# Two diffusion-backbone layers on one core: the experts as one run of slices, the pair gather inside the pair ahead, and identity products in PE's waits

## The reference

```
def _moe(h, router, wg, wu, wd):
    logits = (h @ router).astype(jnp.float32)
    top_v, top_i = lax.top_k(logits, TOP_K)
    w = jax.nn.softmax(top_v, axis=-1)
    combine = jnp.sum(jax.nn.one_hot(top_i, N_EXPERTS) * w[..., None], axis=-2)
    for e in range(N_EXPERTS):
        out = out + combine[..., e:e + 1] * _swiglu(h, wg[e], wu[e], wd[e])
```

## Time and profile before

| | us |
|---|---|
| median of 3 runs | 1887.31 |
| lowest, highest | 1887.2, 1889.62 |
| the profiled execution, its own time | 1881.97 |
| its span on the core | 1880.1 |
| PE busy | 1794.9 (95%) |
| PE weight loads | 1463.5 (78%) |
| DVE busy | 1333.4 (71%) |
| ACT busy | 1049.5 (56%) |
| POOL busy | 121.3 (6%) |

### The profile page before, as it was taken

One profiled execution on the slowest core, in us unless ns is written; L12 is line 12 of the kernel. 1 busy time (PEld: TensorE's weight loads), 2 busy tenths in 40 slices (PEclk: granted clock), 3 DMA queues, 4 the chain that ended last, 5 costly groups with the idle time before them and its releaser, 6 DMA issues.

```text
span 1880.1 us, 21725 instructions
## 1 busy us (share of the span) xinstructions
PE 1794.9 (95%) x8804; PEld 1463.5 (78%) x8804; DVE 1333.4 (71%) x1245; ACT 1049.5 (56%) x989; POOL 121.3 (6%) x128
## 2 busy tenths in 40 slices
PE   4999989999999999887999999999999999999998
PEld 2986578888888878666888888888888888888886
DVE  2478656332333457745989988999888998898988
ACT  3333744222222244454777777777777777777774
POOL 1020900000000012321000000000000000000000
PEclk8999989999999999997999999999999999999999
DMA  8325913522433133654899998999999999999994
GB/s 296 129 90 188 350 63 77 141 90 82 109 95 101 40 118 129 217 210 179 301 374 378 360 375 324 367 375 362 375 328 361 376 360 375 332 360 374 369 368 165
DMA packets 246198, 472.80 MB, mean 251 GB/s; under 512 B 10578, under 2 KB 60596, under 8 KB 246092
## 3 DMA queue, kind: packets, MB, share of 16 engines
q1 hardware_dynamic: 242000, 468.14, 69.9%
q10 hardware_dynamic: 4092, 3.20, 0.6%
HBM read 470.26 MB, written 1.05 MB: 251 GB/s over the span
## 4 chain that ended last, share of the span: by engine, by line
PE 89%; DVE 5%; ACT 2%; DMA 2%; issue 1%; POOL 1%; SPq 0%; ACTq 0%; POOLq 0%; DVEq 0%
PE bank L554 26%; PE bank L556 26%; PE bank L555 26%; DMA raw<-in_ada_w_dram 2%; PE bank L572 2%; DVE parts L1749 1%; PE bank L1116 1%; PE bank L801 1%; PE bank L1063 1%; PE bank L790 1%; PE bank L782 1%; PE bank L1076 1%; ACT parts L1310 1%; PE bank L851 1%; PE bank L733 1%
## 5 line engine op out<-in xcount | busy, mean ns | idle before, releaser
L1764 DVE TENSOR_TENSOR expert_low<-expert_loaded,expert_high 128x2048 fp32r<-128x2048 f32 x336 | 765.5, 2289 | 84.8 <-ACT expert_high L1451 84.5
L1451 ACT ACTIVATE expert_high<-expert_loaded 128x2048 fp32r<-128x2048 f32 x336 | 642.8, 1919 | 194.5 <-PE bank L556 194.5
L554 PE MATMUL bank<-expert_high,XEr 128*128 128x512 f32 x896 | 354.7, 396 | 6.8 <-issue 4.1
L556 PE MATMUL bank<-expert_high,XEr 128*128 128x512 f32 x896 | 349.9, 390 | 0.0
L555 PE MATMUL bank<-expert_low,XEr 128*128 128x512 f32 x896 | 349.6, 390 | 0.0
L1310 ACT ACTIVATE parts<-raw 128x2048 fp32r<-128x2048 f32 (+1 forms) x62 | 113.2, 1831 | 269.8 <-PE bank L556 249.7
L1749 DVE TENSOR_TENSOR parts<-raw,parts 128x2048 fp32r<-128x2048 f32 (+1 forms) x62 | 135.7, 2193 | 136.3 <-ACT parts L1310 136.0
L554 PEld LDWEIGHTS bank<-expert_high,XEr 128*128 128x128 f32 x896 | 168.7, 188 | 42.3 <-issue 9.1
L556 PEld LDWEIGHTS bank<-expert_high,XEr 128*128 128x128 f32 x896 | 168.5, 188 | 35.6
L555 PEld LDWEIGHTS bank<-expert_low,XEr 128*128 128x128 f32 x896 | 168.8, 188 | 33.5
L554 PE MATMUL bank<-expert_high,HTr 128*128 128x512 f32 x448 | 174.5, 390 | 0.0
(11 more groups left out here) (246 smaller groups left out, 2236.6 us busy)
## 6 DMA issues: line engine op xcount, KB each, us to landing
expert_loaded<-in_moe_w_gate_dram SPq DMA_DIRECT2D x112, 1024.0 KB, 5.5
expert_loaded<-in_moe_w_up_dram SPq DMA_DIRECT2D x112, 1024.0 KB, 5.5
expert_loaded<-in_moe_w_down_dram SPq DMA_DIRECT2D x112, 1024.0 KB, 5.2
raw<-in_ada_w_dram SPq DMA_DIRECT2D x28, 1024.0 KB, 7.8
more<-in_ada_w_dram SPq DMA_DIRECT2D x20, 1024.0 KB, 7.8
raw<-in_w_in_dram SPq DMA_DIRECT2D x12, 1024.0 KB, 5.1
raw<-in_ffn_w_gate_dram SPq DMA_DIRECT2D x22, 512.0 KB, 3.9
raw<-in_ffn_w_up_dram SPq DMA_DIRECT2D x22, 512.0 KB, 5.2
```

Of the source, the lines that this page charges most:

```text
L554: nc.tensor.matmul(out, st[0], mv[0], start=start, stop=False)
L556: return nc.tensor.matmul(out, st[1], mv[0], start=False, stop=stop)
L1451: nc.scalar.activation(high[:, m % PARTS, :], loaded[:, at, :], ACT.Copy).then_inc(hi_ready, 1)
L1764: return nc.vector.tensor_tensor(out, a, b, op)
```

## The change

- **One run of experts.** The four pairs of 14 slices become one run of 56 (`slices`), with items and semaphore counts numbered through. The order within a slice is kept. The end of a pair is gone as a place of its own.
- **The gather inside the pair ahead.** `gathers_in` puts the gather of pair p in slices 10 and 11 of pair p-1: in slice 10 its left half (16 products) between the turn and up, in slice 11 its right half, both into banks M. ACT brings the left half out in slice 10, DVE the right half in slice 11, and the second half of the high and low parts is made in slice 12. The first pair's gather stays ahead of the experts.
- **Identity products.** `keep_busy` issues n plain products of the identity by itself (128x128, float32) into a bank that nobody reads: 9 ahead of the last values of each attention, then 8 (layer 0) or 11 (layer 1); in the routing chain 8 ahead of the second tile's turn, 6 behind it, 11 ahead of the ranks, 5 ahead of the first gather, 9 behind it.
- **POOL** waits ahead of its first `xnr` until DVE has emptied the bank of the second tile's turn.

```diff
+            def keep_busy(out, n):
+
+                for _ in range(n):
+                    nc.tensor.matmul(out, ident, ident, start=True, stop=True)
...
+                    if m == last + 1:
+                        spare = (turn_v[0] + 1) % ring_v[0]
+                        pe.wait_ge(v_done, user_v[spare] + 1)
+                        keep_busy(VB[spare][:, 0:P], 9)
                     if m >= 2:
                         values(2 * m - 4)
                         values(2 * m - 3)
+                    if m == last + 1:
+                        keep_busy(VB[spare][:, 0:P], 8 if layer == 0 else 11)
...
                     if t:
+                        keep_busy(b[:, P:2 * P], 8)
                         turn_routed(1, banks)
+                        keep_busy(b[:, P:2 * P], 6)
...
                 b = open_v()
+                keep_busy(b[:, P:2 * P], 11)
                 after(mask_ready)
...
+        def gathers_in(g):
+
+            p, at = divmod(g, 2 * EF_SLICES)
+            return p + 1, at - TURN_IN if p + 1 < PAIRS else -1
...
+                def gather(p, right):
+
+                    if p:
+                        pe.wait_ge(scatter_read, 4 * e0 + 8 * p - 3)
+                    if p and right:
+                        pe.wait_ge(xe_lo, part * PAIRS + p + 1)
+                    for k in range(4 * right, 4 * right + 4):
+                        out = (M[(k % 4) // 2] if p else (G, U, M[0], M[1])[k // 2])[:, (k % 2) * 2 * P:(k % 2 + 1) * 2 * P]
...
+                def slices():
+                    for g in range(SLICES):
+                        n = 6 * g - 2 if g else 0
                         gate_or_up(g, n, G, gate_half, gate_full)
-                        if g == 1 and opening:
+                        if g == 1:
                             pe.wait_ge(places_read, PAIRS * (part + 1))
-                        if g >= 1:
+                        if g:
                             turn(g - 1)
+                        p, step_ = gathers_in(g)
+                        if step_ in (0, 1):
+                            gather(p, step_)
                         gate_or_up(g, n + 2, U, up_half, up_full)
...
-                    else:
-                        turn(PAIR_SLICES - 1)
-                        gather(i + 1)
-                        down(PAIR_SLICES - 1, n)
...
                 pe.wait_ge(a_done, d_a[0])
+                if not part:
+                    keep_busy(M[0][:, 0:P], 5)
                 pe.wait_ge(places, 2 * part + 1)
                 pe.wait_ge(xn_lo, TT)
-                gather(0)
-                pair(0, True)
-                for i in range(1, PAIRS):
-                    pair(i, False, i == PAIRS - 1)
+                gather(0, 0)
+                gather(0, 1)
+                if not part:
+                    keep_busy(T[0][:, 0:P], 9)
+                slices()
...
+            pool.wait_ge(v_done, job[("turned_low", 1)] + 1)
             for t in range(TT):
                 after(xn_hi)
                 nc.gpsimd.tensor_tensor(xnr[:, 1, t, :], xn[:, t, :], xnr_f[:, 0, t, :], ALU.subtract).then_inc(xn_lo, 1)
```

More of the change, by code:

```diff
@@ new lines, in weights, with gate_or_up @@
+                def weights(m):
+                    pe.wait_ge(lo_ready, BASE + part * ITEMS + m + 1)
+                    return [w.rearrange("p (k n) -> p k n", n=SLICE) for w in (high[:, m % PARTS, :], low[:, m % WEIGHTS, :])]
+                def gate_or_up(g, n, b, half_used, full):
+                    e = g // EF_SLICES
+                    if g:
+                        pe.wait_ge(gate_read if b is G else up_read, s0 + g)
+                    for half in range(2):
+                        hi, lo = weights(n + half)
+                        if g % EF_SLICES == 0 and b is G:
+                            pe.wait_ge(xe_ready, 2 * (e0 + e) + half + 1)
+                        for kk in range(4):
+                            k = 4 * half + kk
+                            x = XEr[:, e % 2, :, k, :]
+                            mm = three(b[:, :], (x[:, 0, :], x[:, 1, :]), (hi[:, kk, :], lo[:, kk, :]), k == 0, k == KT - 1)
+                        mm.then_inc(full if half else half_used, 1)
@@ new lines, in turn, with down @@
+                def turn(g):
+                    pe.wait_ge(up_read, s0 + g + 1)
+                    if g >= 2:
+                        pe.wait_ge(ht_ready, s0 + g - 1)
+                    for j in range(4):
+                        mm = nc.tensor.transpose(T[g % 2][:, j * P:(j + 1) * P], HE[:, g % 2, j * P:(j + 1) * P], ident)
+                    mm.then_inc(h_turned, 1)
+                def down(g, n, halves=(0, 1), closing=False):
+                    pe.wait_ge(ht_ready, s0 + g + 1)
+                    for half in halves:
+                        hi, lo = (v.rearrange("p (j h) n -> p j h n", h=2) for v in weights(n + half))
+                        for h in range(2):
+                            for jj in range(2):
+                                j = 2 * half + jj
+                                x = HTr[:, g % 2, :, j * P:(j + 1) * P]
+                                mm = three(Y[h][:, :], (x[:, 0, :], x[:, 1, :]), (hi[:, jj, h, :], lo[:, jj, h, :]),
+                                           g % EF_SLICES == 0 and j == 0, g % EF_SLICES == EF_SLICES - 1 and j == 3)
+                            if closing and half and h == 0:
+                                mm.then_inc(y_left, 1)
+                        mm.then_inc(down_done if half else down_half, 1)
@@ L1151, in pair @@
[L1151 to L1159 removed]
+                        for e, t in scattered_in(g):
+                            scatter(e, t)
@@ L1161, in scatter_last @@
+                        if 0 < g < SLICES - 1:
+                            down(g - 1, n + 4)
+                    down(SLICES - 2, ITEMS - 4, (0,))
+                    turn(SLICES - 1)
+                    down(SLICES - 2, ITEMS - 4, (1,))
+                    down(SLICES - 1, ITEMS - 2, closing=True)
                 def scatter_last():
@@ new lines, in turned, with slices @@
+                def turned(g):
+                    act.wait_ge(h_turned, s0 + g + 1)
+                    if g >= 2:
+                        act.wait_ge(down_done, s0 + g - 1 + CREDIT)
+                    nc.scalar.activation(HTr[:, g % 2, 0, :], T[g % 2][:, :], ACT.Copy).then_inc(ht_hi, 1)
+                def slices():
+                    for g in range(SLICES):
+                        n = items_in(g)
+                        split_expert(n[0], part)
+                        act.wait_ge(gate_full, s0 + g + 1)
+                        if g >= 2:
+                            act.wait_ge(up_read, s0 + g - 1)
@@ L1504, in pair @@
                             expert_in_high(1, 0)
                             expert_in_high(1, 1)
-                        more = 4 if g == 0 or g == PAIR_SLICES - 1 else 6
-                        for m in range(n + 1, n + more):
-                            split_expert(i, m, part)
-                        n += more
-                        if g == 0 and opening:
+                        for m in n[1:]:
+                            split_expert(m, part)
+                        if g == 0:
                             for q in range(PAIRS):
@@ L1514, in pair @@
                                                      ACT.Copy).then_inc(places_read, 1)
-                        if g == EF_SLICES:
-                            expert_high(i, 0)
-                    turned(PAIR_SLICES - 1)
-                    if not closing:
-                        gathered(i + 1)
-                gathered(0)
-                pair(0, True)
-                for i in range(1, PAIRS):
-                    pair(i, False, i == PAIRS - 1)
-                expert_high(PAIRS, -1, True)
+                        if g and g % EF_SLICES == 0:
+                            expert_high(g // EF_SLICES - 1)
+                    turned(SLICES - 1)
+                gathered_left(0)
+                gathered_right(0)
+                slices()
+                expert_high(N_EXPERTS - 1, True)
             att_base = 0
```

266 lines of the change are left out of this document (98 added, 168 removed).

## The result

The changed kernel takes 1874.38 us in the median of six runs (1870.27 to 1875.27), the kernel before 1887.06 in six runs beside them (1886.18 to 1889.62): a ratio of 0.9928 (0.9918 to 0.9939), or 12.7 us less. The forecast was 10.7 less.

A forecast was written before the change was run, and what follows sets the result against it. PE, busy for 95% of the span, was taken as the bound. Gains of 4.1 + 5.9 + 1.2 + 1.8 = 13.0 us, less one slow stretch of 2.3, gave 10.7: 1876.6 us for the median, range 1871.0 to 1882.0.

The forecast's parts named there:

- The pair boundary: Between expert pairs: three PE idle times of 1.38 us go, 4.1 us gained, nothing lost for moving the gather.
- The margin in slice 10: In slice 10 the next item is ready at 9.2 us, PE uses it at 10.7: 1.5 us to spare.
- The second rival: The gather in slice 10 makes PE wait, 1.4 us in each of three pairs: 1880.7 us; chance 0.18 with the fourth.
- the fourth: The boundary's wait reappears at an expert pair's first slice: 1880.7 us; chance 0.18 together with the second rival.
- POOL's wait: In the routing chain: with POOL held back, the second `xn` ends earlier and the turn starts 2.0 us sooner.
- its rule on two SBUF inputs: A DVE instruction with two SBUF inputs contends with POOL reading SBUF; the moved subtractions block the choice of experts, 1.65 us.
- The chain: Routing chain at full clock, with the choice of experts blocked: the first expert starts 5.9 us earlier.
- the likeliest case: One slow stretch of PE's clock, 2.3 us, or a short second one: gain 10.7, 1876.6 us; chance 0.52.
- The first expert's products: Six or seven products at the first expert's start no longer run at clock 0.50: 1.2 us gained.
- Layer 1's `project_out`: End of layer 1's attention: twelve products take 2.8 instead of 4.6 us, all behind follows PE: 1.8 us gained.
- The identity products: In PE's waits: 0.21 to 0.22 us each, all fit at full clock and cost nothing; at half clock every group overshoots.
- the third rival: Identity products don't hold the clock and become the bound, mean above 0.33 us each: 1888.8 us; chance 0.08.

The follow-up runs named there:

- experiment 1: The changed kernel without its identity products and without POOL's wait, leaving only the run of experts: 1881.56 us, ratio 0.9972 to the kernel before.
- experiment 2: The changed kernel without its identity products, POOL's wait and the run of experts kept: 1875.86 us, ratio 0.9939 to the kernel before.
- experiment 6: The changed kernel without the identity products at the ends of both attentions, those of the routing chain kept: 1874.53 us, ratio 0.9929 to the kernel before.
- experiment 11: The changed kernel without the identity products at the end of layer 0's attention, all others kept: 1874.44 us, ratio 0.9931 to the kernel before.
- experiments 4 and 7: 4: changed kernel with POOL's second subtraction behind the choice of experts, 1874.25 us; 7: changed kernel with the routing chain's identity products doubled, 1877.47 us.
- experiment 3: The changed kernel without POOL's wait, identity products and run of experts kept: 1874.94 us, ratio 0.993 to the kernel before.
- experiment 9: Changed kernel with both subtractions on DVE, and layer 1's `fold_rows` (short products) moved behind the next tile's twelve products: 1871.24 us, ratio 0.992.

## Why the prediction was right

It was right in sign and size (1876.6 forecast, 1874.38 measured, inside 1871.0 to 1882.0), and by its own steps it was right in part by luck, through errors that cancel.

- **The pair boundary: right mechanism, mis-sized.** The step "What goes is the idle: 3 x 1.38 = 4.1 us" should have read 5.9. Idle time as the timeline gives it is not what the wait costs: from start to start it is 1.54 us, and the products behind it are slower. Both could be read in the earlier trace rows and the rows around it. The margin in slice 10 held, and its count was close: 9.2 us were reckoned from the turn to the low part, and 9.2 measured. The second rival (a wait in slice 10) and the fourth (the wait at a pair's first slice) are out: 965.00 of 965.00 us busy.
- **POOL's wait: right as a mechanism, mis-sized in what hangs on it.** The prediction read the 2.82 us of `xn` as a case of its rule on two SBUF inputs. That operation has one tensor input and a scalar for each partition, so it shows only that DVE ended when POOL did; the choice, with two inputs, is the row that bears on the rule. `xn` came down to 0.75, and the choice was blocked, 1.65 us reckoned and 1.5 measured (1.83 against 0.36). What I did not see is that this one line also wins without the identity products: 5.7 us in the median between experiments 1 and 2, in the profiles half of it in the chain and half behind the first expert's first product, where experiment 1 had a longer slow stretch than the kernel before.
- **The chain: 5.9 reckoned at full clock throughout, 5.0 measured** with one slow stretch, at 884.6 to 887.9, under the five identity products and the gather (4.91 us instead of 4.07). One slow stretch is what the likeliest case assumed, and it lay where the prediction looked for it, behind PE's idle ahead of the ranks. Its price is read on DVE, which had ended its two splits and waited 1.27 us for the gather: 1.3 us, where 2.3 had been taken off. Without it the chain would have won 6.3.
- **The first expert's products: 1.2 reckoned, 1.0 measured** (985.36 before against 984.34 with the pairs kept). It scatters: behind the same chain it was 3.0 in experiment 1 (981.39 against 978.39).
- **Layer 1's `project_out`: the step that failed.** "All behind it follows PE, so 1.8 us": the products did gain 1.7, and 1.6 were given back at 843 to 847. Experiment 6 puts the whole at 0.15. The forecast counted a slow stretch as cured where it had only moved. Layer 0 was reckoned at nothing, and experiment 11 finds nothing.
- **The identity products: right in price, wrong in worth.** One takes 0.26 us in the mean, not the 0.33 and more that the third rival needs. They did not hold the clock everywhere: in experiments 4 and 7 the first group ran at 0.50 for 3 us. And the argument treated them as what makes the chain fast, while on top of the rest they are worth 1.5 us in the median (experiment 2, with ranges that overlap), in the traces 2.1, in the chain (29.00 against 26.87). Most of their gain was also to be had from POOL's wait.

By medians the 12.7 us are 5.7 for the run of experts (experiment 1), 5.7 for POOL's wait on top of it (experiment 2) and 1.5 for the identity products on top of both; the 0.2 by which this is above 12.7 lies between two sets of runs of the kernel before. In another order POOL's wait is worth 0.6 (experiment 3), so the last two are one term of 7.2 that can't be split without naming the order. Of the forecast's 10.7, the boundary was 1.8 too low, the chain with its slow stretch 1.4 too low (3.6 against 5.0), the first products 0.2 and the attention of layer 1 1.65 too high: with the measured sizes it is 5.9 + 5.0 + 1.0 + 0.15 = 12.1, which is what the pieces of the two traces give without the first.

From the second scaling of `xn` to the first expert it is 20.8 us (872.72 to 893.51), "about 20" in the prediction, 25.8 before.

## What to carry to other kernels

Price a wait from start to start of the instructions around it, not by its idle time, and look at the pitch of those behind it. Before you fill waits with products to keep the clock, remove what causes the waits: the subtractions moved from POOL to DVE's own idle time gained 2.2 to 2.8 us, where all the identity products gave 1.5 to 2.1, and took a slow stretch with them. What the identity products are worth on top of that was not run. And where a slow stretch is cured, look for it further on before the gain is counted, in several runs, since it can move or come back by chance.

## What the runs showed of the hardware

- **Tiny DVE operations can become long beside POOL.** Beside a POOL subtraction on 128x1024, a DVE scaling of 128x1024 took 2.82 us instead of 0.75, two operations on 128x8 took 1.83 instead of 0.36, four on 128x128, beside a subtraction and the clearing of `ACC`, 3.17 instead of 1.11. Each ended 0.1 to 0.7 us behind an operation of POOL; a reduction with one input beside the same subtraction stayed at 0.17. The number of tensor inputs does not decide alone: the scaling and the four have one too.
- **PE's clock can fall while PE is busy.** It went to 0.50 with PE busy for 1.00 of each us (843 to 847 after), behind turns and 16-column products; and in experiments 4 and 7 right behind 8-column logits, so that plain 128x128 products without a gap ran at 0.50 for 3 us. The Trainium skill ("TensorE: Matmul & The Clock Gate", Part 4, PE-mode transpose) says that the full clock doesn't engage for transposes, which don't count as busy in the same way. No run here separates turns from short products; in experiment 9 twelve products at 1.00 stood between the two, and the clock fell only behind the short ones.
- **The slow stretches scatter.** The kernels before and after, which up to 758 us differ in layer 0's identity products alone, differed there by two slow stretches in places of their own, and were 3.9 us apart in one pair of profiles; experiments 1 and 2, which are the same up to there, were 3.4 apart. Five to ten runs of one kernel lie within 2 to 5.5 us of each other, fifteen of the kernel before within 10. Differences under about 2 us are told here by pieces of traces, or not at all.
